# Moving the rests of the dense heads' query weights from VectorE to GpSimd, between the halves of a decoding

## The reference

```python
h  = rmsnorm(x)
z  = h @ w_in                      # projections of two attention groups
x += concat(FoX out, MLA out) @ w_o
x += PEER(rmsnorm(x))              # product-key retrieval over 128^2 experts
y  = rmsnorm_final(x)

def _peer(...):                    # a block of 128 rows, 8 heads
    q  = (xb @ w_pq) per head, normalised
    s1 = q[:128] . keys1;  s2 = q[128:] . keys2
    v1, i1 = top_k(s1, 16);  v2, i2 = top_k(s2, 16)
    sv, si = top_k(v1[:, None] + v2[None, :], 16)
    e  = i1[si // 16] * 128 + i2[si % 16];  g = softmax(sv)
    act = gelu(peer_u[e] . xb) * g;  out = act @ peer_v[e]
```

## Time and profile before

| | us |
|---|---|
| median of 3 runs | 1928.15 (1927.27 to 1930.62) |
| the profiled execution | 1932.49, span 1930.7 |
| busy in the span: TensorE, VectorE, GpSimd, ScalarE | 1764.2, 1613.6, 978.8, 803.5 |
| the 16 rests of head 0 to 7 on VectorE | first at 355.9, last at 489.9 |
| the dense heads' queries on TensorE | 358.8 to 501.4 |

### The profile page before, as it was taken

The page is one execution under the profiler, slowest core; times in us unless marked ns, Lnnn a source line. Parts: engine busy times, 40 slices in busy tenths (PEclk is TensorE's granted clock), DMA queues, the critical chain, the costliest instruction groups (busy, mean ns, idle before and its releaser), DMA issues.

```text
span 1930.7 us, 28368 instructions
## 1 busy us (share of the span) xinstructions
PE 1764.2 (91%) x9239; PEld 1483.0 (77%) x9239; DVE 1613.6 (84%) x3321; ACT 803.5 (42%) x1314; POOL 978.8 (51%) x779
## 2 busy tenths in 40 slices
PE   6999899888959877569999999999999999999998
PEld 4883454677628776459989998999899989998997
DVE  5205463489879799989999999999999999999999
ACT  4312562344316655434344344434444443444343
POOL 0004000024340023267777777777777777777773
PEclk7999999898879988779999999999999999999999
DMA  6110303233114444289999999999999999999996
GB/s 250 44 64 2 131 1 125 93 125 106 70 51 146 171 146 138 81 322 416 416 392 400 400 392 392 401 408 392 395 411 392 392 405 399 398 395 409 393 393 272
DMA packets 169006, 517.87 MB, mean 268 GB/s; under 512 B 18129, under 2 KB 51857, under 8 KB 164849
## 3 DMA queue, kind: packets, MB, share of 16 engines
q0 software_dynamic: 73728, 268.47, 34.9%
q1 hardware_dynamic: 70448, 223.46, 30.5%
q10 hardware_dynamic: 24768, 25.17, 3.8%
HBM read 486.20 MB, written 30.84 MB: 268 GB/s over the span
## 4 chain that ended last, share of the span: by engine, by line
PE 76%; DVE 17%; ACT 4%; issue 2%; DMA 1%; SPq 0%; ACTq 0%; DVEq 0%
PE ps L1297 28%; PE ps L1313 9%; PE ps L1315 9%; PE ps L1314 9%; PE ps L1146 3%; DVE asel L1585 2%; DVE bsel L1578 2%; PE ps L985 2%; PE ps L987 2%; PE ps L986 2%; PE ps L1185 1%; PE ps L1234 1%; DVE wpql L1337 1%; PE ps L1105 1%; PE ps L1012 1%
## 5 line engine op out<-in xcount | busy, mean ns | idle before, releaser
L628 POOL DMA_INDIRECT ubuf<-in_peer_u,ix x256 | 387.0, 1512 | 156.2 <-POOL ix L673 109.1
L628 POOL DMA_INDIRECT vbuf<-in_peer_v,ix x256 | 397.6, 1553 | 78.9 <-issue 77.7
L1313 PE MATMUL ps<-hh,uh 128*128 128x384 f32 x1024 | 346.8, 339 | 17.8 <-DVEq L1706 17.8
L1315 PE MATMUL ps<-hh,ul 128*128 128x384 f32 x1024 | 345.8, 338 | 0.0
L1314 PE MATMUL ps<-hl,uh 128*128 128x384 f32 x1024 | 344.4, 336 | 0.0
L1718 DVE SCALAR_TENSOR_TENSOR ubuf<-ubuf,h2Y 128x1024 f32<-128x1024 f32 x256 | 302.6, 1219 | 0.8 <-issue 0.7
L931 ACT ACTIVATE vh<-vb 128x1024 fp32r<-128x1024 f32 x128 | 136.0, 1062 | 304.2 <-PE ps L1297 295.9
L1297 PE MATMUL ps<-vl,acth 128*128 128x512 f32 x774 | 243.1, 395 | 0.0
L1297 PE MATMUL ps<-vh,actl 128*128 128x512 f32 x774 | 242.5, 394 | 0.0
L1297 PE MATMUL ps<-vh,acth 128*128 128x512 f32 x774 | 242.5, 394 | 0.0
L1313 PEld LDWEIGHTS ps<-hh,uh 128*128 128x128 f32 x1024 | 193.9, 189 | 24.2 <-issue 18.6
(11 more groups left out here) (367 smaller groups left out, 2961.6 us busy)
## 6 DMA issues: line engine op xcount, KB each, us to landing
ub<-in_peer_uT SPq DMA_DIRECT2D x130, 512.0 KB, 6.7
vb<-in_peer_v SPq DMA_DIRECT2D x129, 512.0 KB, 6.5
gbuf<-gate_matrix SPq DMA_DIRECT2D x68, 384.0 KB, 8.2
gate_matrix<-stage ACTq DMA_DIRECT2D x12, 2048.0 KB, 7.8
wpqX<-in_wpq SPq DMA_DIRECT2D x8, 1024.0 KB, 5.3
wpqY<-in_wpq SPq DMA_DIRECT2D x8, 1024.0 KB, 5.0
w_oX<-in_w_o SPq DMA_DIRECT2D x4, 1024.0 KB, 7.9
kTs<-in_past_k SPq DMA_DIRECT2D x8, 512.0 KB, 3.9
```

The lines of the kernel that those rows point to most:

```text
L628: nc.gpsimd.indirect_dma_start(out=dst[slot][:, e, :], out_offset=None, in_=t_in[table], in_offset=bass.IndirectOffsetOnAxis(ix[:, slot, e ...
L1313: mm(ps[:, 6 + slot, 0:NTD], uh[slot][:, k], hh[:, k], start=(k == 0), stop=False)
L1315: last = mm(ps[:, 6 + slot, 0:NTD], ul[s][:, k], hh[:, k], start=False, stop=(k == KD - 1))
```

## The change

VectorE keeps the rests of head 0 alone. GpSimd makes those of heads 1 to 7 with the same subtraction, in a loop over heads: it first adds the new keys of sample h, and, for h = 4 and 6, puts the two rests of head h between `second_keys` and `first_keys` of pair h/2 - 2. The last two pairs' decodings follow the loop, as before. The waits for the rounding (`wpq_rounded`) and the semaphore that TensorE waits on (`wpq_split`) are the same ones; GpSimd first waits until head 0's rests are counted.

```diff
--- before.py
+++ after.py
@@ -636,12 +636,26 @@
                         gather(dst, table, s, e, done)
 
             pool.wait_ge(o_copied, PAIRS)
+
+            def low_weights(h):
+                for c in range(2):
+                    at = (slice(None), slice(None), slice(c * P, (c + 1) * P))
+                    pool.wait_ge(wpq_rounded, 2 * h + c + 1)
+                    nc.gpsimd.tensor_tensor(wpq_lo[h % 2][at], GR[0].wpq[h % 2][at], wpq_hi[at].bitcast(F32),
+                                            ALU.subtract).then_inc(wpq_split, 1)
+
             add_new_keys(0)
             add_new_keys(1)
-            for pair in range(PH // 2):
-                for b in range(2 * pair + 2, 2 * pair + 4):
-                    if b < DB:
-                        add_new_keys(b)
+            pool.wait_ge(wpq_split, 2)
+            low_weights(1)
+            for h in range(2, PH):
+                add_new_keys(h)
+                if h >= 4 and h % 2 == 0:
+                    second_keys(0, h // 2 - 2)
+                low_weights(h)
+                if h >= 4 and h % 2 == 0:
+                    first_keys(0, h // 2 - 2)
+            for pair in range(PH // 2 - 2, PH // 2):
                 second_keys(0, pair)
                 first_keys(0, pair)
             for pair in range(PH // 2):
@@ -1628,8 +1642,6 @@
 
 
             row_max(FIRST)
-            low_weights(1, 0)
-            low_weights(1, 1)
             for h in range(1, PH + 1):
                 items = half_choices(0, h - 1)
                 behind_pair = h % 2 == 1 and h > 1
@@ -1637,17 +1649,11 @@
                 if not behind_pair:
                     normalise(FIRST + h - 1)
                 else:
-                    if h + 1 < PH:
-                        low_weights(h + 1, 0)
                     copy_out(FIRST + h - 2)
                 some(items, 8)
-                if not behind_pair and h + 1 < PH:
-                    low_weights(h + 1, 0)
                 some(items, 4)
                 if not behind_pair and h >= 2:
                     copy_out(FIRST + h - 2)
-                if h + 1 < PH:
-                    low_weights(h + 1, 1)
                 some(items, 4)
                 if h < PH:
                     row_max(FIRST + h)
```

## The result

The changed kernel took 1936.5 us, the median of four runs (1935.58 to 1938.42), beside 1928.17 us of the kernel before, also four runs (1927.27 to 1930.62): a ratio of 1.0037 (95% interval 1.0024 to 1.0049); the medians lie 8.3 us apart. Run again beside 23 runs of the kernel before, it took 1935.98 against 1930.89 us, a ratio of 1.0024 (1.0015 to 1.0033), the medians 5.1 us apart. The forecast was 1932.9, range 1927.0 to 1939.0, with 0.61 on slower.

The account below looks back on a forecast made before the run. VectorE's order of work was taken to pace two pairs of heads; the new order delays each by 2.7 us, together 5.4, less 0.7 given back: 4.7 us on 1928.15, forecast 1932.9 us, range 1927.0 to 1939.0.

Parts of the forecast that it names:

- Heads 0 to 3 count nothing: Before the first decoding: VectorE's saving in heads 1 to 3 only lengthens its wait for ScalarE's exponential; 0 us.
- A rest of 2.35 us: GpSimd's subtraction, taken from its same-size multiplication: 2.35 us, bounds 1.23 and 4.79.
- The ring's length, 11.36 us: Heads 4 and 6: half a decoding 8.86, subtraction 2.35, hand-over 0.15 us before TensorE starts, 3.49 us later than before.
- The first half of the queries, 6.1 us: TensorE in heads 4 and 6: slow start falls wholly into the queries, 0.9 and 0.2 us more.
- the 2.7 forecast for the first of the two pairs: Second pair's delay: 3.49 later start plus 0.9 slower queries less 1.69 spare at the exponential, 2.7 us.
- The tail, -0.7: Behind the third pair's choices: TensorE's shorter wait and faster clock give back 0.7 us, bounds 0 and 2.4.
- The sum: Whole kernel: 5.4 us of delay in two pairs less 0.7 given back, 4.7 us later.
- The lock: GpSimd's subtraction holding up a VectorE instruction; only a rival counted it, 2.35 us once a pair.
- the idle time at the exponential: Inside the next pair's choices: VectorE arrives over 4 us before head 4's exponential ends.
- Faster by 14.8 us, with the rests in time: Both bound pairs: VectorE's relief counts in full, 7.4 us each, 1913 us; chance 0.10.
- Slower still, by a dear subtraction or by a lock on VectorE's path: Both pairs: subtraction of 4.79 us adds 4.9, or VectorE held 2.35 a pair adds 4.7; chance 0.14.
- No change, with the clock paying back: Heads 4, 6 and behind: no slow start in queries, 2.4 us regained; -0.5 us, 1927.6; chance 0.10.

Follow-up runs that it names:

- the two moves of the rests: Both rests of heads 4 and 6 put ahead of, or behind, both halves of the decoding, against the changed kernel: 1925.94 us and 1953.45 us.
- the added instruction: One more GpSimd multiplication by ones ahead of the first rest of heads 4 and 6, against the changed kernel: 1940.93 us.
- the best version: First rest of heads 4 and 6 ahead of the decoding, second left between its halves, against the changed kernel: 1919.97 us.
- twice the instructions: Six GpSimd multiplications by ones added ahead of both rests of heads 5 and 7 and second rests of 4 and 6, against the changed kernel: 1939.25 us.

## Why the prediction was right, and where its sizes were off

*Heads 0 to 3 count nothing.* They took 419.51 - 356.52 = 62.99 us from head 0's first query to the decoding. Before, head 0 began at 358.84 (the fence of the kernel before, below), and 421.50 - 358.84 = 62.66: 0.3 us off. What VectorE saved there went, as said, into the wait for the exponential: 3.24 us at row 408.89 where 1.49 stood. The decoding came at 419.51, not 421.5, only since head 0 itself came 2.3 us earlier in this execution. The change does not touch the stage ahead; there TensorE was granted 1.00 of its clock from 196.17 to 212.69 us, 16.52 us, and before only 0.85 for the same work from 196.93 to 216.28, 19.35 us. In the repeat of the change and the seven kernels built on it head 0 also begins at 356.2 to 356.9; of the kernel before there is only this one trace.

*A rest of 2.35 us.* 2.34 to 2.42 in all versions, but for the one of 3.63 that a one-hot held up; with the fp32r output, that is as long as the multiplication of the same size without it (2.35 us, row 685.68).

*The ring's length, 11.36 us.* 11.33 and 11.34, and the two moves of the rests and the added instruction shift it as the sum says.

*The first half of the queries, 6.1 us.* This term was mis-sized for head 4: 437.82 - 430.84 = 6.98 us, granted 0.59 of the clock, where before it was granted 0.81 (5.24 us). For head 6 it held: 483.34 - 477.31 = 6.03, granted 0.70 (before 0.72). The prediction's upper bound of 7.7 us follows from rows of the kernel before: granted 0.50 (359.0 to 362.5 us), head 0's first matmuls start 0.32 us apart, granted 1.00 (364.0 to 368.0 us) 0.17, and 24 of them at 0.32 make 7.7. The 0.9 us of head 4 make the difference between the 2.7 forecast for the first of the two pairs and 46.46 - 42.99 = 3.47 measured; for the other, 2.7 was forecast and 45.46 - 42.96 = 2.50 measured.

*The tail, -0.7.* Wrong in sign: from the third decoding's start to the end of the fourth, the last, it took 0.3 us more (578.62 - 511.43 = 67.19 against 574.34 - 507.45 = 66.89). TensorE's wait shrank as forecast (2.74 us; 2.7 was said), and its transposes from 1.51 to 1.12. But the 32 matmuls behind them took 16.54 us (row 520.19), where they took 15.74 before (row 516.54, below). Behind that row stands the granted clock of the same stretch in both (5 us, from 10.5 us behind the third decoding's start; the kernel before first, then the changed one):

```profile
358.84 0.69 PE L1181 MATMUL ps<-hh,wpqh 128*128 128x384 f32 x1 [1.41 <-DVE hl L1337]
...
516.54 15.74 PE L1146 MATMUL ps<-w_oY,oTY 128*128 128x512 f32 x32
```

```profile
518.00:523.00 5.00, 5.00 (x10) 2.00 (x9) 4.85 (x16) 1.13 (x5) 4.76 (x4) 0.79 0.00 0
```

```profile
521.98:526.98 5.00, 5.00 (x9) 2.11 (x8) 4.82 (x17) 1.19 (x5) 4.76 (x4) 0.66 0.01 2
```

The 5 us ahead of this stretch were granted 0.50 in both, and those behind it 1.00; windows of 0.4 us from 505 to 529 us show only these two values in either trace, but for the four windows in which the clock changes (0.54 to 0.66). In between the changed kernel was longer at 0.50, a mean of 0.66 against 0.79, though it had waited less. That gave 0.80 us away, twice what the transposes had won. The low stretch was not longer as a whole (by the windows that follow some 10.2 us in both), it lay later: before, the clock fell inside the wait (granted 0.83 from 509.50 to 510.00) and rose among the matmuls (0.93 from 520.00 to 520.50); in the change it fell in the transposes (0.60 from 515.00 to 515.50) and rose among the matmuls too (0.66 from 525.00 to 525.50). Behind the third decoding's start both came 1.3 us later, so less of the low stretch fell into idle time and more into the matmuls. That a shorter wait would pay in clock was an assumption, and here it did not hold.

*The sum.* In the heads 0.3 + 3.47 + 2.50 + 0.3 = 6.6 us where 4.7 was forecast. The profiled spans differ by 3.2, since the changed execution was 2.3 us earlier ahead of the heads and 1.1 shorter behind them (1933.9 - 578.62 = 1355.3 us against 1930.7 - 574.34 = 1356.4); both lie within what one kernel's runs differ by (the kernel before ran from 1927.0 to 1933.0 us). The forecast's 4.7 lies in the intervals of both measurements, 4.6 to 9.4 and 2.9 to 6.4 us. The path was foreseen; that the repeat came as near as 5.1 is in part luck, since the sum of the heads was 1.9 too small.

*The lock.* The forecast's sum has no term for it; a rival had it at 2.35 us a pair. It met VectorE's normalisation, where row 431.26 shows 5.42 us for 0.63, and was covered. Row 423.78 had shown it on a subtraction with two input tensors (3.60 us for 1.23); normalisation has one tensor and a column, the conversion of row 416.77 one input (2.29 us for 0.26), and both were held as well. The experiments set the limit of the cover: it was the idle time at the exponential, 3.25 and 3.28 us (the prediction had over 4), and there is none between VectorE's last index and the one-hots: at row 416.77 the hold delayed them by 2.0 us.

*The rivals.* Faster by 14.8 us, with the rests in time: this was not the change's order, but it is what the order asks for, and the best version has 38.48 and 39.08 us a pair, 8.4 less than the kernel before in both together. Slower still, by a dear subtraction or by a lock on VectorE's path, was not the case here: the first is excluded by the 2.34 to 2.42 us, the second by the waits that rows 444.38 to 500.88 still show. No change, with the clock paying back, fell with head 4's 6.98 us and the tail.

## What to carry to other kernels

Before work goes to an engine with a lighter load, follow what it waits for in that engine's order and who waits for it in turn: the same fourteen subtractions made the kernel 1953, 1936, 1926 or 1920 us by their place alone, and a VectorE busy 98% of a pair (41.94 of 42.99 us) said nothing of that. Give each piece the place that its own consumer needs; here the first rest belonged ahead of the decoding and the second between its halves. And look on which instruction of VectorE a GpSimd instruction will fall, and how long VectorE waits behind it anyhow: in these kernels that wait was all that hid it (3.25 us idle in the change, none left at row 455.79 with twice the instructions, and the time 3.3 us longer).

## What was not expected of the hardware

A short VectorE instruction stood for nearly the whole of a GpSimd instruction that it met, and the next one for the next: of two normalisations the first stood 1.92 us until a rest was over and the second 3.57 us until the multiplication behind it was, and small operations of 0.26 us took 2.29 beside a rest of 2.38 (row 416.77) and of 2.36 (row 417.92). And TensorE's slow start did not grow with the wait ahead of it: head 4's first half of queries took 6.98 us behind 6.87 us of idle time in the change (6.99 behind 6.90 in its repeat), 5.89 us behind 9.33 with the doubled instruction, and 6.67 us behind 14.30 with the rests last. What sets its length no run here shows.
